# The first expert's tokens found ahead of the router's lists, and the gates moved into the first expert: a two-layer decoder trunk on one Trainium2 core

## The reference

```python
coarse_prob = softmax(t @ w_coarse + b_coarse)
p_top, g_top = lax.top_k(coarse_prob, 1)
fine_logits = (t @ w_fine + b_fine)[group g_top]
f_val, f_idx = lax.top_k(fine_logits, 2)
gate = p_top * softmax(f_val)
expert_idx = g_top * 4 + f_idx
out = sum over the two experts e of gate_e * ((silu(t @ w_gate[e]) * (t @ w_up[e])) @ w_down[e])
```

## Time and profile before

| what | value |
|---|---|
| median of 3 runs | 1426.92 us (1425.71 to 1427.56) |
| the profiled execution, its own time | 1426.11 us |
| its span, first to last instruction | 1424.3 us |
| PE busy | 1354.9 us, 95% |
| DVE busy | 1005.6 us, 71% |
| ACT busy | 787.0 us, 55% |
| POOL busy | 205.9 us, 14% |
| mean granted clock of TensorE | 0.975 |

### The profile page before, as it was taken

One profiled execution on the slowest core, in us unless ns is written; L12 is line 12 of the kernel. 1 busy time (PEld: TensorE's weight loads), 2 busy tenths in 40 slices (PEclk: granted clock), 3 DMA queues, 4 the chain that ended last, 5 costly groups with the idle time before them and its releaser, 6 DMA issues.

```text
span 1424.3 us, 20559 instructions
## 1 busy us (share of the span) xinstructions
PE 1354.9 (95%) x7135; PEld 1118.3 (79%) x7135; DVE 1005.6 (71%) x1350; ACT 787.0 (55%) x977; POOL 205.9 (14%) x309
## 2 busy tenths in 40 slices
PE   7999977999999999999999999999997799999995
PEld 6888866888888877888888788888776688888883
DVE  6656477999899996252558535344966799999998
ACT  5222253888888853533357252325724488888882
POOL 3000021111111302020200111120002111111131
PEclk9999987999999999999999999999998799999998
DMA  5238425999999964232210222231025699999994
GB/s 208 89 120 314 173 99 204 372 388 388 393 392 386 384 238 165 68 111 89 90 60 2 89 90 93 87 116 60 2 95 208 223 382 385 395 386 391 383 352 177
DMA packets 85089, 307.88 MB, mean 216 GB/s; under 512 B 12145, under 2 KB 12169, under 8 KB 68644
## 3 DMA queue, kind: packets, MB, share of 16 engines
q1 hardware_dynamic: 75936, 291.19, 55.0%
q0 software_dynamic: 8640, 15.86, 2.9%
q10 hardware_dynamic: 452, 0.02, 0.0%
HBM read 291.19 MB, written 31.46 MB: 227 GB/s over the span
## 4 chain that ended last, share of the span: by engine, by line
PE 87%; DVE 6%; issue 3%; ACT 2%; DMA 1%; POOLq 0%; SPq 0%; DVEq 0%; POOL 0%; ACTq 0%
PE ps L324 26%; PE ps L326 25%; PE ps L325 25%; PE ps L1853 2%; PE ps L1634 1%; PE ps L1836 1%; DVE probT L1428 1%; PE ps L1928 1%; PE ps L1535 1%; DMA x_rows<-hn_rows,tok_list 1%; DVE h L1210 1%; PE ps L1818 1%; ACT W_hi L725 1%; PE ps L1821 1%; PE ps L1649 1%
## 5 line engine op out<-in xcount | busy, mean ns | idle before, releaser
L324 PE MATMUL ps<-W_hi,xT_hi_all 128*128 128x512 f32 x1408 | 559.5, 397 | 3.3 <-DVE rope_b L1496 1.5
L326 PE MATMUL ps<-W_hi,xT_lo_all 128*128 128x512 f32 x1408 | 551.0, 391 | 0.0
L325 PE MATMUL ps<-W_lo,xT_hi_all 128*128 128x512 f32 x1408 | 549.2, 390 | 0.0
L1139 DVE TENSOR_TENSOR W_lo<-m_raw,W_hi 128x2048 fp32r<-128x2048 f32 x192 | 435.9, 2291 | 58.4 <-ACT W_hi L725 56.3
L725 ACT ACTIVATE W_hi<-m_raw 128x2048 fp32r<-128x2048 f32 x192 | 367.1, 1914 | 47.9 <-PE ps L326 47.5
L324 PEld LDWEIGHTS ps<-W_hi,xT_hi_all 128*128 128x128 f32 x1408 | 265.1, 188 | 63.8 <-issue 7.2
L326 PEld LDWEIGHTS ps<-W_hi,xT_lo_all 128*128 128x128 f32 x1408 | 264.9, 188 | 57.5
L325 PEld LDWEIGHTS ps<-W_lo,xT_hi_all 128*128 128x128 f32 x1408 | 265.5, 189 | 51.6
L680 ACT ACTIVATE W_hi<-raw,mix_gain 128x512 fp32r<-128x512 f32 x192 | 123.0, 712 | 290.7 <-issue 278.7
L954 DVE SCALAR_TENSOR_TENSOR W_lo<-raw,mix_gain,W_hi 128x512 fp32r<-128x512 f32 x192 | 132.5, 752 | 211.4 <-ACT W_hi L680 208.7
L646 POOL TENSOR_TENSOR qk_rot<-rope_a,rope_b 128x512 f32<-128x512 f32 x48 | 62.2, 1300 | 365.4 <-DVE rope_b L1496 365.4
(11 more groups left out here) (245 smaller groups left out, 1409.6 us busy)
## 6 DMA issues: line engine op xcount, KB each, us to landing
m_raw<-in_w_gate_dram SPq DMA_DIRECT2D x64, 1024.0 KB, 7.7
m_raw<-in_w_up_dram SPq DMA_DIRECT2D x64, 1024.0 KB, 8.4
m_raw<-in_w_down_dram SPq DMA_DIRECT2D x64, 1024.0 KB, 7.4
raw<-in_attn_w_qkv_dram SPq DMA_DIRECT2D x36, 1024.0 KB, 5.0
raw<-in_conv_w_in_dram SPq DMA_DIRECT2D x12, 1024.0 KB, 5.2
y_rows<-zero_rows SPq DMA_DIRECT2D x2, 4096.0 KB, 17.4
y_pick<-y_rows SPq DMA_DIRECT2D x16, 512.0 KB, 7.4
raw<-in_conv_w_out_dram SPq DMA_DIRECT2D x4, 1024.0 KB, 7.6
```

The costliest lines, as they stand in the source:

```text
L324: pe.matmul(o, a_hi, b_hi, start=first, stop=False)
L325: pe.matmul(o, a_hi, b_lo, start=False, stop=False)
L326: return pe.matmul(o, a_lo, b_hi, start=False, stop=last)
L1139: dve.tensor_tensor(MW_lo[c % MSPLIT][:, :, :], m_raw[c % MRAW][:, :, :], MW_hi[c % MSPLIT][:, :, :].bitcast(F), ALU.subtract).then_inc(s[ ...
```

## The change

The change has three parts, made in both layers.

- **The first token column.** When PE has the counts of earlier tokens (`prefix_done`, new), DVE copies those of expert 0 (`first_pos`), and makes four one-hots of 128 tokens x 128 lanes, masked by who uses expert 0 (`first_oh`). PE multiplies each with the token numbers into one PSUM column (four products of 1 column in f32). DVE writes this as `tok_col`, before the general one-hots. POOL's first gather reads `tok_col` and no longer waits for the lists; POOL waits for them behind it.
- **The gates.** The terms of the gates now come behind `rows_lo` of the first item, the gate values behind the split of unit 2. The split of unit 1 moves behind the terms of the gates. The two exponentials on ACT come behind `rows_hi` of the first item. The copy of the gate list to SBUF moves behind the split of unit 5.
- **The gates' list.** The eight products of `list_gates` on PE move from ahead of unit 0 to behind unit 3.

Three unused semaphores are dropped and two are added.

```diff
+        first_oh = at("first_oh", [P, NT, P], F, FG + 14 * KB)
+        first_pos = temp("first_pos", [P, NT])
...
             def moe_rows(l):
                 s = M[l]
 
-                pool.wait_ge(routed, 2 * l + 2)
+                pool.wait_ge(first_ready, 3 * l + 3)
                 pool.wait_ge(x_zeroed, l + 1)
...
-                                        bass.IndirectOffsetOnAxis(ap=tok_list[:, 0:1], axis=0),
+                                        bass.IndirectOffsetOnAxis(ap=tok_col[:, 0:1], axis=0),
                                         bounds_check=S - 1, oob_is_err=False
                                         ).then_inc(s["rows_in"], 16)
+                pool.wait_ge(routed, 2 * l + 2)
...
             def experts_begin(l):
...
-                act.wait_ge(ex_in, 2 * l + 1)
-                act.activation(t4[:, :, :], t4[:, :, :], ACT.Exp).then_inc(ex_out, 1)
-                act.wait_ge(ex_in, 2 * l + 2)
-                act.activation(ex[:, :], ex[:, :], ACT.Exp).then_inc(ex_out, 1)
...
                 rows_hi(0, FIRST_X)
+                act.wait_ge(ex_in, 2 * l + 1)
+                act.activation(t4[:, :, :], t4[:, :, :], ACT.Exp).then_inc(ex_out, 1)
+                act.wait_ge(ex_in, 2 * l + 2)
+                act.activation(ex[:, :], ex[:, :], ACT.Exp).then_inc(ex_out, 1)
                 m_hi(l, 3, 0)
...
+                dve.wait_ge(prefix_done, l + 1)
+                after(dve.tensor_copy(first_pos[:, :], ps[:, 5, 0:64].rearrange("p (r e) -> p r e", r=NT)[:, :, 0]))
+                for r in range(NT):
+                    ins = dve.tensor_scalar(first_oh[:, r, :], iota_f[:, :], first_pos[:, r:r + 1],
+                                            used[:, r, 0:1].bitcast(F), ALU.is_equal, ALU.mult)
+                ins.then_inc(first_ready, 1)
+
                 dve.wait_ge(pos_done, l + 1)
...
                 after(dve.tensor_tensor(cand_f[:, :, :], cand_f[:, :, :], lane_i[:, :, :], ALU.subtract))
+                dve.wait_ge(first_ready, 3 * l + 2)
+                dve.tensor_scalar(tok_col[:, :], ps[:, 4, 0:1], float(2 * S), None, ALU.add).then_inc(first_ready, 1)
                 for c in range(2):
...
                 dve.tensor_scalar(tok_list[:, :], dest_list[:, :], 2 * S + S - 1, None, ALU.bitwise_and
                                   ).then_inc(routed, 1)
 
+                m_lo(l, 0, 0)
+
+            def gate_logits(l):
...
-                m_lo(l, 0, 0)
+
+            def gate_values(l):
+
                 dve.wait_ge(ex_out, 2 * l + 1)
...
-                m_lo(l, 1, 0)
...
                 rows_lo(0, FIRST_X)
+                gate_logits(l)
+                m_lo(l, 1, 0)
                 m_lo(l, 2, 0)
-                dve.wait_ge(s["gate_listed"], 1)
-                dve.tensor_copy(gate_list[:, :], ps[:, 7, 0:CAND]).then_inc(s["gate_copied"], 1)
+                gate_values(l)
                 m_lo(l, 3, 0)
                 m_lo(l, 4, 0)
                 rows_lo(1)
                 act_mul(0, 3, 6)
                 m_lo(l, 5, 0)
+                dve.wait_ge(s["gate_listed"], 1)
+                dve.tensor_copy(gate_list[:, :], ps[:, 7, 0:CAND]).then_inc(s["gate_copied"], 1)
...
-                    pe.matmul(ps[:, 5, NE * (q + 1):NT * NE], ones_r[:, :],
...
+                ins.then_inc(prefix_done, 1)
 
                 pe.wait_ge(used_ready, 2 * l + 2)
                 pe.matmul(ps[0:CAND, 6, 0:2], row_counts[:, :, :].rearrange("p e j -> p (e j)"), ones_r[:, 0:2],
                           start=True, stop=True).then_inc(pos_done, 1)
+                pe.wait_ge(first_ready, 3 * l + 1)
+                for r in range(NT):
+                    ins = pe.matmul(ps[:, 4, 0:1], first_oh[:, r, :], dest_id[:, 0, r:r + 1], start=(r == 0),
+                                    stop=(r == NT - 1))
+                ins.then_inc(first_ready, 1)
                 pe.wait_ge(valid_ready, l + 1)
...
                 turn_x(0)
-                list_gates()
                 pe.wait_ge(s["xlo"], 1)
...
                 turn_x(1)
                 up_unit(3, 0, 3, xh0, xl0, 5)
+                list_gates()
                 pe.wait_ge(routed, 2 * l + 2)
```

More of the change, by code:

```diff
@@ L272, in build @@
         x_in = [sem(f"x_in{r}") for r in range(NT)]
-        sp_passed, pool_passed, dve_passed = sem("sp_passed"), sem("pool_passed"), sem("dve_passed")
+        sp_passed, pool_passed = sem("sp_passed"), sem("pool_passed")
         pos_in, conv_in = sem("pos_in"), sem("conv_in")
@@ L279, in build @@
         split_hi, split_lo, unit_done = sem("split_hi"), sem("split_lo"), sem("unit_done")
-        pool_step, dve_step, act_step = sem("pool_step"), sem("dve_step"), sem("act_step")
+        pool_step, dve_step = sem("pool_step"), sem("dve_step")
         consts_ready, rows_ready, trig_ready, trig_done = (
             sem("consts_ready"), sem("rows_ready"), sem("trig_ready"), sem("trig_done"))
-        conv_t, conv_taps = sem("conv_t"), sem("conv_taps")
+        conv_t = sem("conv_t")
         ssq_ready, rstd_ready, hn_ready, h_ready = sem("ssq_ready"), sem("rstd_ready"), sem("hn_ready"), sem("h_ready")
@@ L308, in build @@
             sem("rank_done"), sem("item_oh_ready"), sem("items_done"))
-        routed = sem("routed")
+        routed, prefix_done, first_ready = sem("routed"), sem("prefix_done"), sem("first_ready")
         zero_ready, zeroed, x_zeroed = sem("zero_ready"), sem("zeroed"), sem("x_zeroed")
@@ L1112, in route @@
                                   ).then_inc(routed, 1)
+                m_lo(l, 0, 0)
+            def gate_logits(l):
+                fours = lg[:, :, :].rearrange("p r (g e) -> p (r g) e", e=4)
+                fine = lg[:, :, NG:20].rearrange("p r (g e) -> p r g e", g=NG)
                 after(dve.tensor_reduce(best[:, :, :].rearrange("p r g -> p (r g)"), fours, AX.X, ALU.max))
@@ L1600, in router @@
                 for q in range(NT - 1):
-                    pe.matmul(ps[:, 5, NE * (q + 1):NT * NE], ones_r[:, :],
-                              used[:, q, :].unsqueeze(1).to_broadcast([P, NT - 1 - q, NE]), start=False,
-                              stop=(q == NT - 2))
+                    ins = pe.matmul(ps[:, 5, NE * (q + 1):NT * NE], ones_r[:, :],
+                                    used[:, q, :].unsqueeze(1).to_broadcast([P, NT - 1 - q, NE]), start=False,
+                                    stop=(q == NT - 2))
+                ins.then_inc(prefix_done, 1)
                 pe.wait_ge(used_ready, 2 * l + 2)
```

## The result

The changed kernel takes 1418.85 us (1417.31 to 1419.55, 4 runs) against 1427.24 (1425.71 to 1427.91, 4 runs) for the kernel before: ratio 0.9944, 95% interval 0.9932 to 0.9955. It is faster by 8.4 us. The profiled execution took 1418.97, with a span of 1417.0 where it was 1424.3.

A forecast was written before the change was run, and what follows sets the result against it. PE was taken to bound the loop. Unit 0 6.2 earlier less 1.3 gave 4.9, rounded to 5.0 a layer, 10 for two: 1426.1 - 10.0 = 1416.1, plus 0.8 is 1416.9, forecast 1417.0; range 1414.5 to 1423.0, forecast's own 1414.5 to 1419.5.

The forecast's parts named there:

- What bounds the kernel: Loop over items: PE sets its fixed length, so unit 4 starting 1 us earlier ends the layer 1 us earlier.
- When the gather starts: Router to POOL's first gather: starts at 214.5 in place of 217.89, 3.4 earlier.
- How long the gather takes: First gather: without waiting for DVE's split it lands 4.7 after its start, bounds 4.2 and the old 6.37.
- Rival 1: First gather: as slow as before, still 6.37, costing 1.7 of the 5.0 a layer; 1420.3, chance 0.22.
- From landing to unit 0: Rows' landing to unit 0: takes 3.6, no longer held by the gates' list; unit 0 at 222.8, 6.2 earlier.
- From unit 0 to unit 4: First item's units: with the same slow stretches, the gates' list brings unit 4 1.3 later after unit 0 than before.
- Rival 2: PE's clock at unit 0: rises late, slow stretch 8.8 instead of 3.4, 2.7 more lost a layer; 1422.4, chance 0.07.
- Who else must be in time: DVE, ACT and loads beside PE: all in time, unit 3's split on DVE with a slack of 1.0.
- Rivals 3 and 4: 3: weights' loads or DVE's queue take most gain, 1425.0, chance 0.08; 4: POOL starved by DVE, 1429.1, chance 0.05.

The follow-up runs named there:

- the fourth experiment: Changed kernel with unit 0's split moved right behind the token column's write, beside the gather: 1419.55 us, ratio 0.995 to the kernel before.
- the gates alone: Changed kernel without the token column: first gather by the general list again, gates and their list in their new places; 1425.83 us, ratio 0.9997 to the kernel before.
- the warm turn: Changed kernel plus seven dense products into an unused PSUM bank, two before the first turn, five behind; 1417.09 us, ratio 0.9932 to the kernel before.
- the one-pass column: Changed kernel with the first column's one-hots and token numbers in fp32r, two columns per product: 1418.57 us, ratio 0.9938 to the kernel before.

## Why the prediction was right, and where not

The forecast was 1417.0 and the kernel takes 1418.85: the direction and the mechanism held, and the error of 1.85 lies well inside the range. The total flatters the sum. The forecast was built from a profiled execution and gave 10.0 less; the two profiled executions lie 7.1 apart (1426.11 and 1418.97), 2.9 short. The medians lie 8.4 apart (and the one before came at 1427.24 in place of 1426.92), since the profiled execution of the kernel before was one of its faster ones and that of the changed kernel one of its slower. That the total came within 1.85 is in part the luck of these draws.

**What bounds the kernel**: right. Unit 4 comes 7.1 sooner in all, by the measure above, and the span is 7.3 shorter.

**When the gather starts**: 214.5 forecast, 214.97 found. The trace's router began 0.2 later. The column's products took 1.88 where I took 1.7, the one-hots 1.12 where I took 1.0. Both were inside their bounds. What mattered was to price a one-column f32 product like one with 64 columns and the same stationary tile: it was 0.47 each, against 0.43.

**How long the gather takes**: right, and shown from both sides. I took 4.7; it was 4.59 and 4.91. Taking the split away in the kernel before brings POOL from 3.18 to 1.29, and putting it beside the gather in the changed kernel brings it from 1.29 to 2.45. In three kernels POOL ends 1.16 after the split in layer 0. Rival 1 (the price of a first gather) falls with these. One case I had not seen: the gather began 1.0 after the split in the fourth experiment and was still held for the rest of it, and then needed almost its whole own time. The gates alone show the same. The short operations on VectorE between which the changed kernel's gather runs cost it nothing that these traces show: 1.29 is also what it took in the kernel with the split moved away.

The Trainium skill (SBUF — State Buffer, on the port pair that VectorE and GpSimd share) has the later engine locked out for the whole of the earlier one's operation. For the split the trace agrees, with 3.18 against 1.29: 1.9 more, where the split still ran for 2.0. For the one-hots, which have two inputs in SBUF too, it does not: in layer 0 the gather took its 1.29 among them, and they start as far apart beside it (214.57, 215.03) as before without it (212.71, 213.16).

One reading of this step was wrong for layer 1. "The loads of units 4 and 5 don't stand in the way" was read from 215 to 216 in layer 0. In layer 1 of the changed kernel the DMA share is 0.97, 1.06 and 0.96 from 1099 to 1102, with the gather under way from 1099.60. It took 4.91, where with the split moved away it took 4.26, started at 1104.19, with a share of 0.00 from 1104 to 1105. The 4.7 of the sum was high enough to hide this.

**From landing to unit 0**: right. 3.6 forecast, 3.63 found (219.60 to 223.23), and DVE was free 0.9 before it was asked. Unit 0 came 5.8 earlier, 6.2 was forecast, and the 0.4 is that of the gather's start.

**From unit 0 to unit 4**: this is the step that failed. "With the same slow stretches" took 4.1 and 2.7 at the low clock over from the kernel before. They were 6.0 and 5.1. Half of the difference, 0.95 and 1.2, is lost, 2.15 in all. That is most of the 2.9 by which the profiled executions fall short; unit 0 (6.0 and 6.1 earlier by the measure from `used`, and not 6.2) and the rounding from 4.9 to 5.0 make up 0.5 more. The gates' list itself was right: 1.73 where I took 1.7. What I had costed at nothing is what stands ahead of unit 0: the list, 3.43 of work, was replaced by 2.4 of idle time between the turn and unit 0. That this is what moved the rise is likely but only in part shown. Rival 2 named this mechanism and gave it 8.8 and a chance of 0.07. The measured time lies between it and the forecast, nearer to the forecast.

How much of it is the move and how much the draw of this one profile is not settled. Unit 0 to unit 4, with the list counted and the waits of 0.4 taken off, is 14.9 on average over the six layers of three kernels with the list ahead (14.3 to 15.5), and 15.75 over the ten of five kernels with it behind and no warm products (15.0 to 16.5). The ranges overlap. So about 0.85 a layer goes with the list's place on average, and the rest is spread. The clock itself rose 1.8 to 4.2 after unit 0 in the six layers and 2.9 to 6.0 in the ten. One pair speaks against the list's place as the only cause: in the gates alone the list is behind too, and the clock rose 2.9 and 3.1 after unit 0, no later than before. The other eight layers with the list behind, at 3.5 to 6.0, have the early gather as well, and no run separates the two. The warm turn shows the cause from the other side, that work in these gaps brings the rise nearer: seven products in the idle time and nothing else changed bring the stretch to 0.5 or less, and unit 0 to unit 4 from 16.5 and 16.05 to 14.9, of which 0.85 is a new wait. The Trainium skill (TensorE: Matmul & The Clock Gate, Part 1) has the moment of the rise shift from run to run; the runs show a spread too, with 2.9 to 6.0 among the ten layers with the list behind, and 2.4 and 4.2 in the two layers of the one kernel with its split moved later.

**Who else must be in time**: right. The slack at unit 3's split was put at 1.0 and was 1.8, larger since PE was slower. Its price showed when PE became faster: a wait of 0.83 and 0.86 in the warm turn.

**Rivals 3 and 4**: both fall. The gain of unit 4 arrives in the total, and POOL got its turn among the one-hots at once. The expectation that the two parts would not add up was met most plainly: 0.8 and 2.1 alone, 8.4 together.

## What to carry to other kernels

Where two chains end at nearly the same time, shortening either alone gives next to nothing, so price the pair, and look for what the removed piece did besides its work. Here products that seemed only to be in the way also kept TensorE busy before the real work. Kernels without them there took about 0.85 a layer more (between groups whose ranges overlap, and which differ in more than this), and a handful of idle products gives it back. Look too at what runs beside an indirect DMA's instruction on GpSimd: a 2.3 us two-input operation on VectorE costs it up to 1.9, and moving one line undid that (0.28% of the kernel).

## What the runs showed of the hardware that was not expected

- Idle products pay only where they fit. Seven of them around the turn brought 0.9944 to 0.9932, some 1.7 us; the intervals overlap, and it is the trace, with unit 4 at 28.8 and 30.1 after `used` and not at 30.55 and 30.35, that shows the gain in layer 0. In layer 1 the slower gather took nearly all of it. 39 over the whole router gained nothing more than the changed kernel has (0.9946 and 0.9944): the first sixteen took 5.25 and 6.67 us in place of 3.6, for the most part at the low clock, and pushed back the path behind them.
- An earlier gather can land no earlier. In layer 1, with POOL on it for 1.11 each time, it took 4.91 from 1099.60, 4.99 from 1099.99, 5.37 from 1098.95, 5.44 from 1098.44 and 5.84 from 1099.27 while the loads of units 4 and 5 were under way, and the turn began 4.5 after its start with the load of unit 5 held back. It took 4.26 from 1104.19 with the queues empty. The loads are the likely cause; the one run that holds a load back has the one-pass column and the warm products too.
- Four f32 products with one column took 1.88, the same four in fp32r with two columns 1.01, both at a granted clock of 0.50.
